# Moving a context norm one tile earlier and splitting its weight unit in two, in a two-block transformer kernel

## Chip, cores and metric

The kernel runs as one program on 1 core of one Trainium2 chip. The metric is device time in microseconds (us) of one launch; the median of the runs is compared.

## The reference, cut to what matters

A sequence of 512 rows of 1,024 channels goes through `first_block` (two layers, each attention and a gated feed-forward part of width 2,816) and `second_block`. All is computed in fp32. What the change touches is the border between the blocks:

```python
    return rmsnorm(x, g_final)                       # end of first_block
...
    h = modulate(rmsnorm_2(x, g_pre1[l]), sh1, sc1)      # second_block, x is that result
    hc = modulate(rmsnorm_2(ctx, g_pre1[l]), csh1, csc1) # ctx: 256 rows x 1024, an input
    q, k, v, f, g_a, g_f = split_proj(h @ w_in[l])
    pc = hc @ w_in[l, :, :Q_W + 2 * KV_W]                # only its k and v columns are used
```

## The kernel before, in words

Activations lie transposed in SBUF: 8 chunks of 128 channels by 512 rows. Every weight goes through one stream of units. For each unit the SP queue loads it into `raw` (2 slots), ScalarE (ACT) rounds it into `w_hi`, GpSimd (POOL) forms the rest `w_lo`, and TensorE (PE) forms three products per pair of 128x128 weights and activation chunk (hi by hi, hi by lo, lo by hi). `hi_unit` (L595) waits for the matmuls of the unit two before it; `L565` is POOL's part, `L1502` and `L1524` are the products. A unit is ready for PE when POOL has counted it (`unit_ready`).

The down projection `dn11` ends the first block: 8 units of 1,408 columns, each one output chunk of 33 matmuls. After each unit VectorE (DVE) adds the residual (L1175) and sums squares of the chunk twice: weighted, for the norm `pre1` (L1135, L1144), and plain, for the final norm (L1186 to L1189). The norm of the context is put among these units. In the ACT program, `context_rows`, and in DVE's, `context_part`, say what is done behind unit u: squares and their sum at u=1, a ones matmul on PE behind unit 2 (`context_sum`), root and inverse at u=3, and scaling, rounding (`ctx_hi`, L841) and rest (`ctx_lo`, L1161) from u=3 on. In `context_rows` each `next_hi` (the rounding of unit u+1) stands ahead of the context work of u, so work of u that waits for DVE delays the rounding of unit u+2.

Then comes the unit `ctx` (2,048 columns: 128 key and 128 value columns of 8 chunks). PE computes the context keys (24 matmuls of 256 columns), then the sums of the norm `pre1` (L1616, 16 matmuls of one column), the first value row tile (24 of 128 columns), the plain sums of the final norm (L1892, 8), the spread of the inverse of `pre1` over 128 partitions (L1623, 8), the second row tile, the spread of the final inverse (L1900, 8), and then unit 0 of `c_in` (48 matmuls of 512 columns, L1524), each of whose eight steps waits for a chunk `h_lo` of DVE (L996). ACT's `h_hi` (L646) of chunk 1 stands behind the copy of the second row tile (L913), and ahead of chunk 2 stands the rounding of unit 1 of `c_in`. Units 1 and 2 of `c_in` and the second block's attention follow.

Of the kernel before, what the change touches and what calls it, by code (L numbers as in the profile page):

```python
# [26 lines left out]
ACT = mybir.ActivationFunctionType  # L27
# [40 lines left out]
def constants():  # L68
# [14 lines left out]
    for name, head, rot in (("32", 128, 32), ("16", 64, 16)):  # L83
# [31 lines left out]
          ("up10", HALF, 2048, 2), ("dn10", 8, HALF * P, 1), ("up11", HALF, 2048, 2), ("dn11", 8, HALF * P, 1),  # L115
          ("ctx", 1, 2048, 3),
          ("c_in", 13, 2048, [2, 2, 5] + [2] * 10),
# [10 lines left out]
def lay_out(x):  # L128
# [31 lines left out]
    c = x["w_in_2"][0]  # L160
    w["ctx"] = units(c[:, 512:768], 256)
    cq = c[:, :512].reshape(D, 8, 64)[:, pair8].reshape(D, 512)
# [81 lines left out]
def program(nc, wdram, params_d, const_d, axial_d, rows_d, x_d, mem_d, ctx_d, cond_d, pos_d, out_d):  # L244
    ctx = ExitStack()
    with ctx:
# [80 lines left out]
        def bank(b, a=0, z=S):  # L327
            return ps[:, b * S + a:b * S + z]
# [255 lines left out]
        def _(act):  # L584
# [130 lines left out]

            def ffn_up(ph, first):
                def body(i, j):
                    next_hi(ph, i, j)

                    act.wait_ge(conv_ready, 2 * i + (j + 1 + first))  # L720
                    nc.scalar.activation(T[:, 2 + j, :], T[:, j, :], ACT.Silu).then_inc(silu_ready, 1)  # L721
                each_unit(act, ph.n, body)
# [104 lines left out]

            def context_rows():
                act.wait_ge(mod_used, 24)
                act.dma_start(CTXT[:], ctx_d).then_inc(load_ctx, 16)  # L830
                for u in range(8):
                    next_hi(PH["dn11"], u // 2, u % 2)
                    if u == 1:
                        act.wait_ge(load_ctx, 16)
                        nc.scalar.activation(CTXSQ[:], CTXT[:], ACT.Square).then_inc(ctx_squared, 1)
                    if u == 3:
                        act.wait_ge(ctx_summed, 1)
                        nc.scalar.activation(CTXR[:], bank(4, 0, MEM), ACT.Sqrt, bias=cst("eps"), scale=1.0 / D).then_inc(ctx_root, 1)
                    for k in range(3 * (u - 4), min(3 * (u - 3), DC)) if u >= 4 else []:
                        act.wait_ge(ctx_scaled, k + 1)  # L840
                        nc.scalar.activation(CTXH[:, k, :], CTXT[:, k, :], ACT.Identity, bias=MODV[:, k, 1:2]).then_inc(ctx_hi, 1)  # L841

            def ffn(l, first):
                for h in range(2):
                    name = f"dn{l}{h}"
                    mod = 8 * MOD_PHASES.index(name) if name in MOD_PHASES else None
                    if mod is not None:
                        if mod:
                            act.wait_ge(mod_used, mod)
                        load_mod(mod)  # L850
                        load_mod(mod + 1)
                    ffn_up(PH[f"up{l}{h}"], first + h * HALF)
                    if name == "dn11":
                        context_rows()
                        continue
                    if mod is None:
                        stream_only(PH[name])
                        continue
                    for u in range(8):
                        next_hi(PH[name], u // 2, u % 2)  # L860
                        if 2 <= u + 1 < 8:
                            act.wait_ge(mod_used, mod + u)
                            load_mod(mod + u + 1)
# [35 lines left out]
            ph = PH["ctx"]  # L899
            next_hi(ph, 0, 0)  # L900

            def after_pre1_root():
                act.wait_ge(final_summed, 1)
                nc.scalar.activation(ROOTF[:], bank(1, 0, ROWT), ACT.Sqrt, bias=cst("eps"), scale=1.0 / D).then_inc(final_root, 1)
                act.wait_ge(ph.done, 1)
                nc.scalar.activation(CKX[:], bank(2, 0, MEM), ACT.Copy).then_inc(ph.free, 1)
                act.wait_ge(ph.done, 2)
                nc.scalar.activation(CVX[:, 0, :], bank(3, 0, P), ACT.Copy).then_inc(ph.free, 1)

            def beside_pre1(k):  # L910
                if k == 1:
                    act.wait_ge(ph.done, 3)
                    nc.scalar.activation(CVX[:, 1, :], bank(0, 0, P), ACT.Copy).then_inc(ph.free, 1)  # L913
                if k == 2:
                    hi_unit(PH["c_in"], 0, 1)

            norm("pre1", None, None, free=[(PH["up11"].done, 22)], after_root=after_pre1_root, beside=beside_pre1,
# [59 lines left out]
        def _(v):  # L977
            chain = Chain(v, vec_steps)
            step = chain.step

            def norm(name, src, gain, shift=None, dst=(HH, HL), into=None, parts="scaled low", beside=None):
                i, nch, rows, b, s = NORMS[name]
# [20 lines left out]
                for k in range(nch if "scaled" in parts else 0):  # L1003
# [15 lines left out]
                    ins.then_inc(scaled_ready, 1)  # L1019
                    if k == 0 and beside is not None:  # L1020
                        beside()
                    if k >= 1 and "low" in parts:
# [127 lines left out]
            def context_part(u):  # L1150
                if u == 1:
                    v.wait_ge(ctx_squared, 1)
                    step(nc.vector.tensor_tensor(CTXSQ[:, 0:4, :], CTXSQ[:, 0:4, :], CTXSQ[:, 4:8, :], ALU.add))
                    step(nc.vector.tensor_tensor(CTXSQ[:, 0:2, :], CTXSQ[:, 0:2, :], CTXSQ[:, 2:4, :], ALU.add))
                    nc.vector.tensor_tensor(CTXSQ[:, 0, :], CTXSQ[:, 0, :], CTXSQ[:, 1, :], ALU.add).then_inc(ctx_added, 1)
                if u == 3:
                    v.wait_ge(ctx_root, 1)
                    step(nc.vector.reciprocal(CTXI[:], CTXR[:]))
                for k in range(3 * (u - 4), min(3 * (u - 3), DC)) if u >= 4 else []:
                    v.wait_ge(ctx_hi, k + 1)  # L1160
                    nc.vector.scalar_tensor_tensor(out=CTXL[:, k, :], in0=CTXT[:, k, :], scalar=MODV[:, k, 1:2],  # L1161
                                                   in1=CTXH[:, k, :].bitcast(F32), op0=ALU.add,
                                                   op1=ALU.subtract).then_inc(ctx_ready, 1)
                for k in range(3 * (u - 3), min(3 * (u - 2), DC)) if u >= 3 else []:
                    nc.vector.scalar_tensor_tensor(out=CTXT[:, k, :], in0=CTXT[:, k, :], scalar=DER[:, 1, k:k + 1],
                                                   in1=CTXI[:], op0=ALU.mult, op1=ALU.mult).then_inc(ctx_scaled, 1)
# [255 lines left out]

            def final_reciprocal():
                v.wait_ge(final_root, 1)
                nc.vector.reciprocal(INVF[:], ROOTF[:]).then_inc(final_inverse, 1)

            norm("pre1", lambda k: XT[:, k, :], lambda k: DER[:, 0, k:k + 1], shift=lambda k: MODV[:, k, 0:1],
                 beside=final_reciprocal)
            ph = PH["c_in"]
# [57 lines left out]
        def _(pe):  # L1487
# [337 lines left out]
            def context_sum(u):  # L1825
                if u == 2:
                    pe.wait_ge(ctx_added, 1)
# [55 lines left out]
            pe.wait_ge(ctx_ready, DC)  # L1883
            advance(t_tiles(ph, 0, (0,), (2,), rows=MEM, ah=CTXH, al=CTXL))
            rows = r_tiles(ph, 0, (0, 1), (3, 0), P, P, ah=CTXH, al=CTXL)

            def final_sums():
                advance(rows, 3 * DC)
                bank_free(1)
                pe.wait_ge(final_added, 1)  # L1890
                for t in range(ROWT):
                    ins = nc.tensor.matmul(bank(1, t, t + 1), T[:, 6, t * P:(t + 1) * P], ONES[:, 0:1], start=True, stop=True)  # L1892
                ins.then_inc(final_summed, 1)

            norm("pre1", after_sums=final_sums)
            advance(rows)
            bank_free(5)
            pe.wait_ge(final_inverse, 1)
            for t in range(ROWT):
                ins = nc.tensor.matmul(bank(5, t * P, (t + 1) * P), INVF[:, t:t + 1].broadcast_to([P, P]), cst("ident", P),  # L1900
                                       start=True, stop=True)
            ins.then_inc(final_spread, 1)
            last_read.update({0: (ph.free, 3), 1: (final_root, 1), 2: (ph.free, 1), 3: (ph.free, 2), 5: (x_ready, XR["final"] + DC)})
            ph = PH["c_in"]
            for u in range(3):
# [8 lines left out]
                else:  # L1914
                    advance(t_tiles(ph, u, (0, 1), (b, b + 1), ready=h_chunk("pre1") if u == 0 else None))
                    last_read[b], last_read[b + 1] = (ph.free, 2 * u + 1), (ph.free, 2 * u + 2)

            def c_rest():
# [93 lines left out]
```

## Time and profile before

| what | value |
|---|---|
| median of 3 runs | 2198.89 us (2198.7 to 2200.43) |
| profiled execution, its own time | 2199.97 us |
| its span, first to last instruction | 2198.2 us |
| PE busy | 2019.5 us, 92% of the span |
| DVE, POOL, ACT busy | 1146.2, 872.0 and 672.7 us |
| mean granted clock of TensorE | 0.963 |

In the timeline a line is one or several instructions of a group: start, time from the start of the first to the end of the last, engine, line, what it writes and reads, how many, and in brackets the idle time ahead of it and what ended it. A matmul's printed time contains its passage through the array, and matmuls overlap; their pace is the distance from start to start. 1.00 is a granted clock of 2.4 GHz, 0.50 is 1.2 GHz.

### The profile page before, as it was taken

How to read it: one execution, taken by the hardware profiler on the slowest of the kernel's cores; microseconds unless marked ns; L12 is line 12 of the kernel's file. 1: busy time of each engine (PE TensorE's matmuls, PEld its weight loads, DVE VectorE, ACT ScalarE, POOL GpSimd, SP SyncE). 2: the span in 40 equal slices, each digit the busy share in tenths (PEclk: the TensorE clock that was granted, in tenths of full speed). 3: DMA queues.
4: the chain of work that ended last, by engine and by line, in shares of the span. 5: the costliest groups of instructions: out<-in, count | busy, mean ns of one | idle time of the engine just before them, and what ended most of it. 6: DMA issues, size and time to landing. Idle time of an engine off the chain costs nothing.

```text
span 2198.2 us, 26021 instructions
## 1 busy us (share of the span) xinstructions
PE 2019.5 (92%) x9702; PEld 1613.7 (73%) x9702; DVE 1146.2 (52%) x2103; ACT 672.7 (31%) x1057; POOL 872.0 (40%) x648
## 2 busy tenths in 40 slices
PE   3988789999899988999999999999998969999997
PEld 3766467788688775567888887878876747888886
DVE  7777874535933766755434435762333455312334
ACT  4232562322122125552221222234434222212211
POOL 4343003444654641115445544442222323444442
PEclk9999999999999998999999999899999979999998
DMA  4222001422532431003325322221110212223221
GB/s 158 76 96 77 25 13 62 163 101 86 219 109 87 184 106 48 25 18 113 121 83 193 131 93 98 100 96 58 58 58 21 87 47 77 89 93 115 96 79 65
DMA packets 32062, 199.15 MB, mean 91 GB/s; under 512 B 3680, under 2 KB 3808, under 8 KB 14048
## 3 DMA queue, kind: packets, MB, share of 16 engines
q1 hardware_dynamic: 27072, 166.74, 21.6%
q10 hardware_dynamic: 4896, 31.15, 3.9%
q8 instruction: 60, 0.98, 0.2%
q14 instruction: 34, 0.28, 0.0%
HBM read 195.78 MB, written 2.10 MB: 90 GB/s over the span
## 4 chain that ended last, share of the span: by engine, by line
PE 49%; DVE 4%; ACT 1%; POOL 1%; issue 1%; DVEq 0%; ACTq 0%
PE psum L1502 42%; PE psum L1524 2%; PE psum L1695 1%; PE psum L1660 1%; PE psum L1677 1%; POOL w_lo L565 1%; PE psum L1952 1%; DVE xT L1012 1%; DVE work L1006 0%; PE psum L1632 0%; ACT w_hi L595 0%; PE psum L1623 0%; DVE work L1188 0%; DVE work L1017 0%; DVE work L1189 0%
## 5 line engine op out<-in xcount | busy, mean ns | idle before, releaser
L565 POOL TENSOR_TENSOR w_lo<-raw,w_hi 128x512 fp32r<-128x512 f32 (+2 forms) x640 | 863.7, 1379 | 1296.9 <-ACT w_hi L595 1296.9
L1502 PE MATMUL psum<-h_hi,w_hi 128*128 128x512 f32 x1560 | 616.0, 395 | 11.8 <-DVE a_q L1048 4.6
L1502 PE MATMUL psum<-h_hi,w_lo 128*128 128x512 f32 x1560 | 612.7, 393 | 0.0
L1502 PE MATMUL psum<-h_lo,w_hi 128*128 128x512 f32 x1560 | 612.4, 393 | 0.0
L595 ACT ACTIVATE w_hi<-raw 128x2048 fp32r<-128x2048 f32 (+2 forms) x176 | 301.6, 1714 | 566.3 <-PE psum L1502 471.9
L1502 PEld LDWEIGHTS psum<-h_hi,w_hi 128*128 128x128 f32 x1560 | 295.0, 189 | 85.1 <-issue 14.4
L1502 PEld LDWEIGHTS psum<-h_hi,w_lo 128*128 128x128 f32 x1560 | 294.7, 189 | 64.1 <-issue 2.4
L1502 PEld LDWEIGHTS psum<-h_lo,w_hi 128*128 128x128 f32 x1560 | 295.0, 189 | 62.4 <-issue 2.3
L1502 PE MATMUL psum<-g_hi,w_hi 128*128 128x512 f32 x528 | 207.5, 393 | 10.4 <-POOL w_lo L565 5.4
L1502 PE MATMUL psum<-g_hi,w_lo 128*128 128x512 f32 x528 | 205.6, 389 | 0.0
L1502 PE MATMUL psum<-g_lo,w_hi 128*128 128x512 f32 x528 | 205.5, 389 | 0.0
L1224 DVE TENSOR_SCALAR work<-psum,params 128x512 f32<-128x512 f32 x66 | 53.5, 810 | 221.0 <-PE psum L1502 212.8
L721 ACT ACTIVATE work<-work 128x512 f32<-128x512 f32 x66 | 41.8, 633 | 401.7 <-DVE work L1228 401.7
L1238 DVE TENSOR_TENSOR work<-psum,work 128x512 f32<-128x512 f32 x66 | 45.7, 692 | 173.9 <-PE psum L1502 170.8
L1502 PEld LDWEIGHTS psum<-g_hi,w_hi 128*128 128x128 f32 x528 | 99.1, 188 | 37.0 <-POOL w_lo L565 8.7
L1122 DVE CUSTOM_DVE_ANT_0 work_flat<-mod_w,conditions 128x1024 f32<-128x1024 f32 x64 | 115.6, 1807 | 1.6
L1502 PEld LDWEIGHTS psum<-g_hi,w_lo 128*128 128x128 f32 x528 | 99.1, 188 | 20.8
L1502 PEld LDWEIGHTS psum<-g_lo,w_hi 128*128 128x128 f32 x528 | 99.1, 188 | 20.1
L1228 DVE SCALAR_TENSOR_TENSOR work<-psum,params,work 128x511 f32<-128x511 f32 (+1 forms) x132 | 98.9, 750 | 15.3 <-DVE work L1224 1.1
L1175 DVE TENSOR_TENSOR xT<-psum,xT 128x512 f32<-128x512 f32 (+1 forms) x48 | 33.2, 691 | 135.0 <-PE psum L1502 134.8
L1524 PE MATMUL psum<-h_hi,w_hi 128*128 128x512 f32 x96 | 43.6, 455 | 50.4 <-DVE h_lo L1264 33.2
L1068 DVE CUSTOM_DVE_ANT_0 work_c<-psum,const 128x512 f32<-128x512 f32 (+1 forms) x32 | 23.0, 755 | 94.8 <-PE psum L1660 94.8
(312 smaller groups left out, 2478.7 us busy)
## 6 DMA issues: line engine op xcount, KB each, us to landing
raw<-w_up SPq DMA_DIRECT2D x66, 1024.0 KB, 4.8
raw<-w_dn SPq DMA_DIRECT2D x48, 704.0 KB, 4.1
mod_w<-w_mod ACTq DMA_DIRECT2D x24, 1024.0 KB, 4.9
raw<-w_c_in SPq DMA_DIRECT2D x13, 1024.0 KB, 4.8
raw<-w_b_in SPq DMA_DIRECT2D x7, 1024.0 KB, 4.8
raw<-w_a_idx SPq DMA_DIRECT2D x5, 1024.0 KB, 5.6
raw<-w_a_out SPq DMA_DIRECT2D x8, 640.0 KB, 3.8
raw<-w_b_out SPq DMA_DIRECT2D x8, 640.0 KB, 3.9
```

What stands on the lines that cost most here:

```text
L565: ins = nc.gpsimd.tensor_tensor(LO[slot][:, a:z], RAW[slot][:, a:z], HI[slot][:, a:z].bitcast(F32), ALU.subtract)
L595: nc.scalar.activation(HI[slot][:, 0:ph.size], RAW[slot][:, 0:ph.size], ACT.Copy).then_inc(hi_ready, 1)
L721: nc.scalar.activation(T[:, 2 + j, :], T[:, j, :], ACT.Silu).then_inc(silu_ready, 1)
L1012: nc.vector.tensor_tensor(XT[:, k, :], XT[:, k, :], out, ALU.add).then_inc(x_ready, 1)
L1068: ins = nc.vector.tensor_tensor_reduce(probs_of(s, n), src, st["mask"], 1.0, PICKED, ALU.add, ALU.max, o[:, n:n + 1])
L1122: ins = nc.vector.tensor_tensor_reduce(TW[:, 4 * S:4 * S + D], MODW[u % 2][:, c, :], COND[:, w, :], 1.0, 0.0, ALU.mult, ALU.add, MODV[:, 2 ...
L1175: nc.vector.tensor_tensor(d, bank(j), d, ALU.add).then_inc(ph.free, 1)
L1224: step(nc.vector.tensor_scalar(t, a, w(mid), w(3), ALU.mult, ALU.add))
L1228: ins = nc.vector.scalar_tensor_tensor(out=t[:, o], in0=a[:, s_], scalar=w(k), in1=t[:, o], op0=ALU.mult, op1=ALU.add)
L1238: nc.vector.tensor_tensor(g, b, T[:, 2 + j, :], ALU.mult).then_inc(ph.free, 1)
L1502: ins = nc.tensor.matmul(out, l, r, start=(k == 0 and m == 0), stop=(k == n - 1 and m == 2))
L1524: ins = nc.tensor.matmul(out, w, a, start=(k == 0 and m == 0), stop=(k == kc - 1 and m == 2))
```

## The change

The unit `ctx` becomes two units of 1,024 columns: keys, then values. The load of the context is issued by ACT ahead of the last SiLU of `up11`, where it stood behind it. Every step of the context norm moves one unit of `dn11` up: squares at u=0, the ones matmul behind unit 1, root and inverse at u=2, and so on. On PE the plain sums of the final norm move behind the second row tile (into bank 6), and the spread of the final inverse moves behind unit 0 of `c_in`. ACT takes the final root at chunk 4 of the norm `pre1`, and DVE the final reciprocal after the norm.

```diff
-          ("ctx", 1, 2048, 3),
+          ("ctx", 2, 1024, [1, 2]),
...
-    w["ctx"] = units(c[:, 512:768], 256)
+    w["ctx"] = units(c[:, 512:768], P)
...
-            def ffn_up(ph, first):
+            def ffn_up(ph, first, last=None):
                 def body(i, j):
                     next_hi(ph, i, j)
+                    if last is not None and isinstance(i, int) and 2 * i + j == ph.n - 1:
+                        last()
...
-            def context_rows():
+            def load_context():
                 act.wait_ge(mod_used, 24)
                 act.dma_start(CTXT[:], ctx_d).then_inc(load_ctx, 16)
+
+            def context_rows():
                 for u in range(8):
                     next_hi(PH["dn11"], u // 2, u % 2)
-                    if u == 1:
+                    if u == 0:
                         act.wait_ge(load_ctx, 16)
...
-                    if u == 3:
+                    if u == 2:
                         act.wait_ge(ctx_summed, 1)
...
-                    for k in range(3 * (u - 4), min(3 * (u - 3), DC)) if u >= 4 else []:
+                    for k in range(3 * (u - 3), min(3 * (u - 2), DC)) if u >= 3 else []:
                         act.wait_ge(ctx_scaled, k + 1)
...
             next_hi(ph, 0, 0)
+            next_hi(ph, 0, 1)
 
             def after_pre1_root():
-                act.wait_ge(final_summed, 1)
-                nc.scalar.activation(ROOTF[:], bank(1, 0, ROWT), ACT.Sqrt, bias=cst("eps"), scale=1.0 / D).then_inc(final_root, 1)
...
                 if k == 2:
                     hi_unit(PH["c_in"], 0, 1)
+                if k == 4:
+                    act.wait_ge(final_summed, 1)
+                    nc.scalar.activation(ROOTF[:], bank(6, 0, ROWT), ACT.Sqrt, bias=cst("eps"), scale=1.0 / D).then_inc(final_root, 1)
```

`context_part` on DVE has the same steps at u one lower, and the reciprocal for the final norm stands behind the norm `pre1`. On PE:

```diff
             def context_sum(u):
-                if u == 2:
+                if u == 1:
...
-            rows = r_tiles(ph, 0, (0, 1), (3, 0), P, P, ah=CTXH, al=CTXL)
-
-            def final_sums():
+            rows = r_tiles(ph, 1, (0, 1), (3, 2), 0, P, width=P, ah=CTXH, al=CTXL)
+
+            def first_rows():
+                unit_ready(ph, 1)
                 advance(rows, 3 * DC)
...
+            norm("pre1", after_sums=first_rows)
+            advance(rows)
+            last_read.update({2: (ph.free, 3), 3: (ph.free, 2)})
+            bank_free(6)
+            pe.wait_ge(final_added, 1)
+            for t in range(ROWT):
+                ins = nc.tensor.matmul(bank(6, t, t + 1), T[:, 6, t * P:(t + 1) * P], ONES[:, 0:1], start=True, stop=True)
...
                     advance(t_tiles(ph, u, (0, 1), (b, b + 1), ready=h_chunk("pre1") if u == 0 else None))
                     last_read[b], last_read[b + 1] = (ph.free, 2 * u + 1), (ph.free, 2 * u + 2)
+                    if u == 0:
+                        final_layout()
```

`final_layout` waits for `final_inverse` and issues the eight matmuls that spread it, which stood ahead of `c_in` before.

## Rows read from the trace of the kernel before

**Rows 1.** The page's chain that ended last, shares of the span by engine.

```profile
PE 49%; DVE 4%; ACT 1%; POOL 1%; issue 1%; DVEq 0%; ACTq 0%
```

**Rows 2.** Timeline of PE, the border of dn11 units 2 and 3, 6, 7, and ctx.

```profile
1363.23 0.39 PE L1502 MATMUL psum<-g_hi,w_lo 128*128 128x512 f32 x1
1365.16 0.70 PE L1829 MATMUL psum<-ctx_squares,ones 128*128 128x256 f32 x2 [1.54 <-DVE ctx_squares L1155]
...
1389.42 0.50 PE L1502 MATMUL psum<-g_hi,w_hi 128*128 128x512 f32 x1 [1.07 <-POOL w_lo L565]
...
1398.04 0.50 PE L1502 MATMUL psum<-g_hi,w_hi 128*128 128x512 f32 x1 [0.85 <-POOL w_lo L565]
...
1405.42 0.39 PE L1502 MATMUL psum<-g_hi,w_lo 128*128 128x512 f32 x1
1408.29 0.39 PE L1502 MATMUL psum<-ctx_hi,w_hi 128*128 128x256 f32 x1 [2.48 <-POOL w_lo L565]
```

**Rows 3.** Timelines of DVE, ACT and POOL over dn11; last the context's load (KB, us to landing).

```profile
1350.67 1.67 DVE L1186 TENSOR_TENSOR work<-xT 128x512 f32<-128x512 f32 x1
...
1362.69 1.23 DVE L1153 TENSOR_TENSOR ctx_squares<-ctx_squares 128x1024 f32<-128x1024 f32 x1
...
1373.49 0.69 DVE L1175 TENSOR_TENSOR xT<-psum,xT 128x512 f32<-128x512 f32 x1 [2.63 <-PE psum L1502]
...
1382.92 0.69 DVE L1175 TENSOR_TENSOR xT<-psum,xT 128x512 f32<-128x512 f32 x1
...
1399.77 0.68 DVE L1175 TENSOR_TENSOR xT<-psum,xT 128x512 f32<-128x512 f32 x1
...
1337.12 0.34 ACTq L830 DMA_DIRECT2D ctxT<-ctx_t  x1
...
1383.46 1.37 ACT L595 ACTIVATE w_hi<-raw 128x1408 fp32r<-128x1408 f32 x1
...
1400.30 1.91 ACT L595 ACTIVATE w_hi<-raw 128x2048 fp32r<-128x2048 f32 x1
...
1384.91 4.45 POOL L565 TENSOR_TENSOR w_lo<-raw,w_hi 128x512 fp32r<-128x512 f32 x3 [5.56 <-ACT w_hi L595]
...
ctxT<-ctx_t ACTq DMA_DIRECT2D x1, 1024.0 KB, 5.2
```

**Rows 4.** Timeline of PE from the context keys to unit 0 of c_in.

```profile
1409.46 0.28 PE L1502 MATMUL psum<-ctx_hi,w_hi 128*128 128x256 f32 x1
...
1412.46 2.15 PE L1616 MATMUL psum<-ones,work 128*128 128x1 f32 x16
1414.48 0.31 PE L1502 MATMUL psum<-w_hi,ctx_hi 128*128 128x128 f32 x1
...
1417.79 1.81 PE L1892 MATMUL psum<-ones,work 128*128 128x1 f32 x8
1419.46 2.05 PE L1623 MATMUL psum<-const,inverses 128*128 128x128 f32 x8
1421.16 0.45 PE L1502 MATMUL psum<-w_hi,ctx_hi 128*128 128x128 f32 x1
...
1426.32 2.02 PE L1900 MATMUL psum<-const,final_inverses 128*128 128x128 f32 x8
```

**Rows 5.** Windows: busy us of PE, PEld, DVE, ACT, POOL (with counts), granted clock, DMA share, GB/s.

```profile
1413.00:1416.40 3.40, 3.40 (x31) 3.40 (x32) 0.18 (x1) 0.26 (x1) 1.53 (x2) 0.98 0.23 41
1416.50:1428.00 11.50, 11.50 (x57) 11.50 (x56) 3.49 (x6) 2.87 (x7) 0.00 (x0) 0.50 0.20 79
1440.80:1467.80 27.00, 26.96 (x168) 24.01 (x167) 20.80 (x32) 4.68 (x5) 12.44 (x8) 1.00 0.22 78
```

**Rows 6.** Timeline of PE: the spread of the inverse in two other norms.

```profile
401.71 1.16 PE L1623 MATMUL psum<-const,inverses 128*128 128x128 f32 x8 [0.57 <-DVE inverses L986]
...
1783.08 2.08 PE L1623 MATMUL psum<-const,inverses 128*128 128x128 f32 x8 [0.56 <-DVE inverses L986]
```

**Rows 7.** Timeline of DVE: the first instruction that waits for unit 0 of c_in.

```profile
1440.20 0.01 DVE L1045 LOAD_MASK_SELECT work<-psum  x1 [1.59 <-PE psum L1524]
```

More of the change, by code:

```diff
@@ L851, in ffn @@
                         load_mod(mod + 1)
-                    ffn_up(PH[f"up{l}{h}"], first + h * HALF)
+                    ffn_up(PH[f"up{l}{h}"], first + h * HALF, load_context if name == "dn11" else None)
                     if name == "dn11":
@@ L912, in beside_pre1 @@
                     act.wait_ge(ph.done, 3)
-                    nc.scalar.activation(CVX[:, 1, :], bank(0, 0, P), ACT.Copy).then_inc(ph.free, 1)
+                    nc.scalar.activation(CVX[:, 1, :], bank(2, 0, P), ACT.Copy).then_inc(ph.free, 1)
                 if k == 2:
                     hi_unit(PH["c_in"], 0, 1)
+                if k == 4:
+                    act.wait_ge(final_summed, 1)
+                    nc.scalar.activation(ROOTF[:], bank(6, 0, ROWT), ACT.Sqrt, bias=cst("eps"), scale=1.0 / D).then_inc(final_root, 1)
             norm("pre1", None, None, free=[(PH["up11"].done, 22)], after_root=after_pre1_root, beside=beside_pre1,
@@ L979, in _, with norm @@
             step = chain.step
-            def norm(name, src, gain, shift=None, dst=(HH, HL), into=None, parts="scaled low", beside=None):
+            def norm(name, src, gain, shift=None, dst=(HH, HL), into=None, parts="scaled low"):
                 i, nch, rows, b, s = NORMS[name]
@@ L1019, in norm @@
                     ins.then_inc(scaled_ready, 1)
-                    if k == 0 and beside is not None:
-                        beside()
                     if k >= 1 and "low" in parts:
@@ L1150, in context_part @@
             def context_part(u):
-                if u == 1:
+                if u == 0:
                     v.wait_ge(ctx_squared, 1)
@@ L1155, in context_part @@
                     nc.vector.tensor_tensor(CTXSQ[:, 0, :], CTXSQ[:, 0, :], CTXSQ[:, 1, :], ALU.add).then_inc(ctx_added, 1)
-                if u == 3:
+                if u == 2:
                     v.wait_ge(ctx_root, 1)
                     step(nc.vector.reciprocal(CTXI[:], CTXR[:]))
-                for k in range(3 * (u - 4), min(3 * (u - 3), DC)) if u >= 4 else []:
+                for k in range(3 * (u - 3), min(3 * (u - 2), DC)) if u >= 3 else []:
                     v.wait_ge(ctx_hi, k + 1)
@@ L1163, in context_part @@
                                                    op1=ALU.subtract).then_inc(ctx_ready, 1)
-                for k in range(3 * (u - 3), min(3 * (u - 2), DC)) if u >= 3 else []:
+                for k in range(3 * (u - 2), min(3 * (u - 1), DC)) if u >= 2 else []:
                     nc.vector.scalar_tensor_tensor(out=CTXT[:, k, :], in0=CTXT[:, k, :], scalar=DER[:, 1, k:k + 1],
@@ L1421, in _ @@
             ffn(1, XT, ("add", "add"))
[L1423 to L1428, printed above, removed]
+            norm("pre1", lambda k: XT[:, k, :], lambda k: DER[:, 0, k:k + 1], shift=lambda k: MODV[:, k, 0:1])
+            v.wait_ge(final_root, 1)
+            nc.vector.reciprocal(INVF[:], ROOTF[:]).then_inc(final_inverse, 1)
             ph = PH["c_in"]
@@ L1883, in _, with final_layout @@
             pe.wait_ge(ctx_ready, DC)
-            advance(t_tiles(ph, 0, (0,), (2,), rows=MEM, ah=CTXH, al=CTXL))
-            rows = r_tiles(ph, 0, (0, 1), (3, 0), P, P, ah=CTXH, al=CTXL)
-            def final_sums():
-                advance(rows, 3 * DC)
-                bank_free(1)
-                pe.wait_ge(final_added, 1)
-                for t in range(ROWT):
[L1892 to L1903, printed above, removed]
+            advance(t_tiles(ph, 0, (0,), (2,), width=P, rows=MEM, ah=CTXH, al=CTXL))
+            last_read[2] = (ph.free, 1)
+            rows = r_tiles(ph, 1, (0, 1), (3, 2), 0, P, width=P, ah=CTXH, al=CTXL)
+            def first_rows():
+                unit_ready(ph, 1)
+                advance(rows, 3 * DC)
+            norm("pre1", after_sums=first_rows)
[5 more added lines that the diff above has]
+                ins = nc.tensor.matmul(bank(6, t, t + 1), T[:, 6, t * P:(t + 1) * P], ONES[:, 0:1], start=True, stop=True)
+            ins.then_inc(final_summed, 1)
+            last_read[6] = (final_root, 1)
+            def final_layout():
+                bank_free(5)
+                pe.wait_ge(final_inverse, 1)
+                for t in range(ROWT):
+                    ins = nc.tensor.matmul(bank(5, t * P, (t + 1) * P), INVF[:, t:t + 1].broadcast_to([P, P]), cst("ident", P),
+                                           start=True, stop=True)
+                ins.then_inc(final_spread, 1)
+                last_read[5] = (x_ready, XR["final"] + DC)
             ph = PH["c_in"]
@@ L1916, in _ @@
                     last_read[b], last_read[b + 1] = (ph.free, 2 * u + 1), (ph.free, 2 * u + 2)
+                    if u == 0:
+                        final_layout()
             def c_rest():
```

## Prediction, on record before the result

> **What bounds the kernel now.** I read the page's chain first [rows 1]. PE carries 49% of the span in the part that is followed and no other engine more than 4%, so a microsecond that PE loses is a microsecond of the kernel, unless another engine paces the stage. Then I read PE's timeline around the diff and looked for its idle brackets. There are four [rows 2]. 1.54 us before the ones matmul of the context norm, which waits for DVE's sum of squares; 1.07 and 0.85 us before units 6 and 7 of dn11; and 2.48 us before the context keys, the last three all waiting for POOL's low parts. Each idle stretch costs about 0.16 us more than its bracket, because matmuls that overlap (start to start 0.227 us) have to fill the array again: from 1405.42 to 1408.29 are 2.87 us where 0.23 would do, 2.64 lost.
>
> Third, the timelines of DVE, ACT and POOL say why POOL is late [rows 3]. From unit 3 on DVE does its residual work and the context's as well. One such round lasts 1382.92 - 1373.49 = 9.43 us with the inverse in it, and the next two (1399.77 - 1382.92)/2 = 8.4 us each, against 33 x 0.227 = 7.5 us of PE for a unit. ACT waits for DVE's scaled context chunks and rounds the next unit only then: at 1383.46, 2.5 us after unit 4 was done. Rounding 1.37 and POOL 4.45 us follow, and PE starts unit 6 late. The ctx unit is the third of these late ones, and the worst: rounding at 1400.30, 1.91 us for 2,048 columns, and four POOL pieces instead of three.
>
> Fourth, from the keys on PE is never idle until c_in, but it isn't always fast [rows 4, 5]. The granted clock is 0.98 between 1413.0 and 1416.4 and 0.50 from 1416.5 to 1428.0, where 128-column matmuls start every 0.213 us, and 1.00 in units 1 and 2 of c_in. There 168 matmuls take 27.0 us; without 72 of 512 columns (16.3 us) that leaves 0.111 us for each of the 96 of 128 columns. So the same matmul costs 0.111 or 0.213.
>
> **The change, step by step.**
>
> *Context load, squares, sum.* The load is issued about 6.4 us sooner (1330.7 for 1337.12) and takes 5.2 us, so it lands at about 1336, ahead of ACT's new square at 1341.6, behind the rounding of unit 1. DVE adds the squares at u=0, from 1350.67 + 1.67 = 1352.34. Alone the three adds take 2.4 us (1362.69 to 1365.1); beside POOL's pieces a DVE operation of this kind takes about 1 us more (1.67 for 0.69), once or twice here: done at 1355.8 to 1356.8, at worst 1357.6. PE asks at 1356.2. I take no wait; the bound is 1.4 us. The 1.54 us and their refill go: -1.7. If DVE were not idle in that round (2.2 us between its end and unit 1), the wait would only move.
>
> *The lag moves one unit up.* Unit 2 is now the one with the inverse behind it. It is done at about 1364.0, and the DVE round that began at 1373.49 begins at 1364.05, 9.44 us sooner. What followed it follows again: late roundings of units 5, 6 and 7. Units 5 and 6 lose what 6 and 7 lost (1.24 and 1.01). Unit 7 takes the place of ctx: rounding at 1400.30 - 9.44 = 1390.86, plus 1.37, 4.45 and 0.14 of handover is 1396.8, against unit 6 done at 1405.65 - 9.44 = 1396.2: 0.6 lost. dn11 ends at 1396.8 + 7.6 = 1404.4, where it ended at 1405.65: -1.2 in all (-1.7, +0.6, rounding).
>
> *The split unit.* Unit ctx 0 is rounded when unit 6 is done, and has half the columns: about 1.1 us of ACT and two POOL pieces of about 1.5, ready at about 1400.5, 4 us ahead of PE. The 2.48 us wait goes: -2.64. Unit ctx 1 may only be rounded when unit 7 is done: 1404.4 + 1.1 + 3.1 = 1408.7. PE wants it after keys and sums, 2.93 + 1.78 = 4.7 us after 1404.4, at 1409.1: no wait, at worst 0.4 with POOL slowed by DVE. The extra activation and DMA lie on ACT and SP, both idle there. ACT then rounds c_in 0 (1.9 us) when the keys are done, and the root of pre1 is queued behind that; the sums take 1.78, so the root is at most 0.3 late, and its result isn't needed for 3 more us. The first row tile covers it.
>
> *Clock of the keys.* Behind the idle 2.48 us the clock fell after a dozen of the 24 key matmuls: 4.17 us from 1408.29 to 1412.46, at a first pace of (1409.46 - 1408.29)/9 = 0.13 with the refill in it [rows 2, 4]. Without the gap I take 24 at 0.118 plus refill, 2.93: -1.24. Bound: 0, if the clock falls anyway. The sums take 16 x 0.111 = 1.78 for 2.02: -0.24.
>
> *Row tile 0.* 3.31 us before (1414.48 to 1417.79), 24 matmuls partly at full clock. The clock fell 4.0 us after the first sum. In two other norms the spread stands 3.3 and 3.6 us behind their first sum, and ran once fast (1.16 us) and once slow (2.08) [rows 6]. I take a fall 3.3 us behind the first sum, so 1.5 us into the tile: 13 x 0.111 + 11 x 0.213 = 3.8 us, +0.5. Bounds 2.67 (all fast) and 5.1 (all slow).
>
> *Plain sums.* They leave the place ahead of the spread: 1419.46 - 1417.79 = -1.67. They come back behind row tile 1, in the place that the final spread leaves (1.67 too), so PE reaches c_in as long after row tile 1 as before.
>
> *Spread and row tile 1.* 1.70 and 5.16 us at half clock, as before: 0.
>
> *Unit 0 of c_in.* ACT's h_hi of chunk 1 is still released by row tile 1, and from there DVE's 1.7 us a chunk set the pace; the end stays 13.8 us behind row tile 1 (1426.3 to 1440.2 [rows 4, 7]). ACT's new root at chunk 4 (0.26 us) fits in its idle of about 1 us a chunk. The final reciprocal comes after DVE's last chunk, 1.5 us before PE wants it. If PE had to wait for it, everything behind would.
>
> *Final spread behind unit 0.* New on the path between units 0 and 1, with nothing beside it: eight matmuls at full clock, 1.16 less the overlap: +1.0 (1.7 at half clock).
>
> Sum: -1.2 - 2.64 - 1.24 - 0.24 + 0.5 - 1.67 + 1.0 = -5.5 us. Behind it PE-bound units and the same attention follow and keep the shift. The profiled execution's 2199.97 (span 2198.2 and 1.8 around it) would become 2194.5; it lies 1.1 above the median, and from the median 2198.89 I get 2193.4.
>
> **A rule that speaks otherwise.** In the trace PE was busy for the whole of 1413.0 to 1416.4 and the clock fell right behind it [rows 5]. The Trainium skill ("TensorE: Matmul & The Clock Gate", "HAM oscillation — how this bites in real kernels") puts the fall down to idle stretches of PE. By that rule the new kernel, which has none behind dn11, would keep the full clock; by the row, a stretch full of one-column and 128-column matmuls is enough for the fall. That is the second case below.
>
> **Rivals.**
> 1. *The clock holds through both row tiles.* For it: 96 such matmuls run at 1.00 in c_in, and the stretch before the sums is now dense. Against: rows 5, a fall with no idle time. Price: row tile 0 2.67, spread 1.0, row tile 1 2.67, so -0.64, -0.7, -2.49 in place of +0.5: -9.8, 2189.1.
> 2. *The clock falls already in the sums.* Row tile 0 takes 5.1 (+1.8), the sums +0.5: -3.4, 2195.5; if the keys are slow too, and the sums take 3.4 us, -1.3, 2197.6. For it: the fall before came at a time that I can't place, and the spread at 1783.08 was slow.
> 3. *The lag isn't moved but grows*: DVE's adds at u=0 hold PE 1.4 us, and ctx 1 is 0.4 late: -3.7, 2195.2.
> 4. *Slower.* The low clock doesn't lift in c_in: each 512-column matmul costs 0.427 for 0.227. It takes 50 of them to turn -5.5 into more than +4.4; for units 0 and 1 together it is about +12, 2211. Against: the window of units 1 and 2 at 1.00, behind a low stretch longer than the new one.
>
> **How the numbers follow.** The forecast's own case (2191.5 to 2195) 50%; rival 1 20%; rivals 2 and 3 24% together; rival 4 and anything like it 6%. 0.2% is 4.4 us, about what a measurement of this kernel tells from no change: 2194.5 and 2203.3. The forecast's case lies below 2194.5 in five of six, rival 1 wholly, rivals 2 and 3 in one of five: faster 0.67, same 0.28, slower 0.05. The range 2188.0 to 2197.6 takes in rival 1 and the bounds of 2 and 3.
>
> **What would show it.** Right: no idle bracket before the ones matmul and before the keys; brackets of about 1.1, 0.85 and 0.4 before units 5, 6 and 7; dn11 ending at about 1404.4; keys in 2.9 us; row tile 1 done at about 1419.8; clock 0.50 there; c_in unit 1 starting 5.5 us sooner. Wrong: a bracket before ctx 1's row tile or the final spread, 128-column matmuls at 0.111 in both tiles, or a shift that is lost behind c_in.

## The result, and the profile after

| | before | after |
|---|---|---|
| median | 2200.43 us (5 runs, 2198.7 to 2204.39) | 2188.43 us (5 runs, 2184.2 to 2193.81) |
| ratio after/before | | 0.9943, 95% interval 0.9922 to 0.9964 |
| profiled execution: span, clock | 2198.2 us, 0.963 | 2182.4 us, 0.972 |

The kernel became 12 us faster; the forecast was 5.5. (Taken from the ratio it is 12.5 us, and its interval goes from 8 to 17.) A second measurement, below, gave 9.2 us.

PE's timeline of the changed kernel, in the places of [rows 2]: the ones matmul, the late units of dn11, and the keys.

```profile
1335.57 0.47 PE L1503 MATMUL psum<-g_hi,w_hi 128*128 128x512 f32 x1 [0.83 <-issue]
...
1351.17 0.70 PE L1830 MATMUL psum<-ctx_squares,ones 128*128 128x256 f32 x2 [0.36 <-DVE ctx_squares L1159]
...
1375.41 0.50 PE L1503 MATMUL psum<-g_hi,w_hi 128*128 128x512 f32 x1 [1.07 <-POOL w_lo L565]
...
1384.03 0.50 PE L1503 MATMUL psum<-g_hi,w_hi 128*128 128x512 f32 x1 [0.85 <-POOL w_lo L565]
...
1392.27 0.50 PE L1503 MATMUL psum<-g_hi,w_hi 128*128 128x512 f32 x1 [0.47 <-POOL w_lo L565]
...
1399.66 0.39 PE L1503 MATMUL psum<-g_hi,w_lo 128*128 128x512 f32 x1
1399.89 0.28 PE L1503 MATMUL psum<-ctx_hi,w_hi 128*128 128x256 f32 x1
...
1402.76 1.84 PE L1617 MATMUL psum<-ones,work 128*128 128x1 f32 x16
1404.52 0.33 PE L1503 MATMUL psum<-w_hi,ctx_hi 128*128 128x128 f32 x1
...
1407.25 1.11 PE L1624 MATMUL psum<-const,inverses 128*128 128x128 f32 x8
1408.11 0.30 PE L1503 MATMUL psum<-w_hi,ctx_hi 128*128 128x128 f32 x1
...
1410.83 1.00 PE L1899 MATMUL psum<-ones,work 128*128 128x1 f32 x8
1411.69 0.48 PE L1525 MATMUL psum<-h_hi,w_hi 128*128 128x512 f32 x1
...
1425.08 1.05 PE L1907 MATMUL psum<-const,final_inverses 128*128 128x128 f32 x8
1425.89 0.48 PE L1503 MATMUL psum<-h_hi,w_hi 128*128 128x512 f32 x1
```

The keys follow dn11 without a gap (1399.66 to 1399.89, where [rows 2] have 2.87 us). The brackets of 1.07 and 0.85 stand one unit earlier than in [rows 2], and a third of 0.47 stands before unit 7. From the keys on, everything is at the fast pace: keys 2.87 us, sums 1.76, row tiles 2.73 and 2.72 (3.31 and 5.16 in [rows 4]), spread and plain sums 0.86 each (1.70 and 1.67). Two windows over this stretch, columns as in [rows 5]:

```profile
1399.90:1411.70 11.80, 11.80 (x106) 11.80 (x104) 7.87 (x9) 5.17 (x9) 8.17 (x6) 1.00 0.33 109
1411.70:1425.90 14.20, 13.08 (x59) 9.51 (x58) 11.20 (x16) 6.85 (x10) 6.38 (x4) 1.00 0.38 142
```

The granted clock is 1.00 where [rows 5] have 0.50.

**How to count.** Of the 15.8 us between the two profiled spans a part lies in code that the change doesn't touch. The clearest place is the attention of the first block's second layer, some 400 us ahead of the change. Windows over the same work, the kernel before first, then after:

```profile
803.00:974.00 171.00, 151.00 (x930) 102.77 (x929) 116.18 (x426) 92.60 (x288) 31.33 (x23) 0.92 0.09 31
```

```profile
802.60:968.70 166.10, 146.08 (x928) 99.73 (x926) 115.56 (x426) 92.44 (x288) 31.32 (x23) 0.95 0.09 32
```

4.9 us there, at a clock of 0.92 and 0.95. Over the 13 profiles of this study dn11 begins anywhere between 1333.6 and 1342.5 us, though the work ahead of it is the same. So I measure the **stage**, from the first matmul of dn11 unit 0 to the first of c_in unit 1, in each profile: 99.68 us before (1340.93 to 1440.61), 90.32 after (1335.57 to 1425.89). The change is worth 9.4 us there, which lies within the interval of 8 to 17. The rest of the first measurement's 12 lies outside the stage, and I put it down to the spread of the executions.

### The profile page after: what moved, and what is told of

It is laid out like the page before. It is cut to its first block, busy times and chain, and to the rows that moved or that the text cites. A ratio compares the mean times of both kernels' runs of the same rounds, so it can differ in the third digit from the quotient of the medians.

```text
span 2182.4 us, 26025 instructions
## 1 busy us (share of the span) xinstructions
PE 2004.0 (92%) x9702; PEld 1599.0 (73%) x9702; DVE 1145.2 (52%) x2103; ACT 672.2 (31%) x1058; POOL 871.9 (40%) x648
## 4 chain that ended last, share of the span: by engine, by line
PE 49%; DVE 4%; ACT 1%; POOL 1%; issue 1%; DVEq 0%; ACTq 0%
PE psum L1503 42%; PE psum L1525 2%; PE psum L1696 1%; PE psum L1678 1%; PE psum L1661 1%; POOL w_lo L565 1%; PE psum L1962 1%; DVE xT L1018 1%; DVE work L1012 0%; PE psum L1633 0%; ACT w_hi L595 0%; PE psum L1624 0%; DVE work L1023 0%; DVE h_lo L1002 0%; PE psum L1617 0%
## 5 line engine op out<-in xcount | busy, mean ns | idle before, releaser
L595 ACT ACTIVATE w_hi<-raw 128x2048 fp32r<-128x2048 f32 (+3 forms) x177 | 301.6, 1704 | 569.3 <-PE psum L1503 474.9
```

Source lines behind the costliest of these rows:

```text
L595: nc.scalar.activation(HI[slot][:, 0:ph.size], RAW[slot][:, 0:ph.size], ACT.Copy).then_inc(hi_ready, 1)
```

## Experiments

Times are medians minus the median of the kernel before, measured beside it on the same chip; the stage is read from each run's one profile. "Tile 0" and "tile 1" are the two value row tiles, and all lengths are in us.

| run | what | idle before keys | keys | tile 0 | tile 1 | stage | time against before, us; ratio's interval |
|---|---|---|---|---|---|---|---|
| before | | 2.48 | 4.17 | 3.31 | 5.16 | 99.68 | |
| after | | 0 | 2.87 | 2.73 | 2.72 | 90.32 | -12.0; 0.9922 to 0.9964 |
| e1 | after again | 0 | 2.88 | 2.74 | 2.71 | 90.27 | -9.2; 0.9946 to 0.9973 |
| e2 | norm up alone | 0.53 | 2.98 | 2.77 | 5.16 | 95.29 | -3.6; 0.9973 to 0.9991 |
| e3 | split alone | 0.56 | 2.94 | 3.24 | 5.16 | 96.16 | -3.4; 0.9969 to 0.9988 |
| e4 | sums last alone | 2.49 | 4.19 | 3.31 | 2.93 | 96.56 | -2.3; 0.9979 to 0.9997 |
| e5 | after without split | 0.51 | 2.98 | 2.92 | 3.32 | 92.67 | -6.5; 0.9954 to 0.9980 |
| e6 | after, old order of sums | 0 | 2.87 | 2.73 | 2.71 | 90.39 | -9.5; 0.9937 to 0.9966 |
| e7 | after, gap of 4.4 | 4.43 | 4.36 | 2.71 | 2.71 | 96.33 | -3.1; 0.9980 to 0.9999 |
| e8 | after, ctx_hi later | 0 | 2.87 | 2.71 | 2.72 | 86.94 | -14.1; 0.9918 to 0.9949 |
| e9 | after, gap of 0.9 | 0.90 | 2.93 | 3.17 | 3.07 | 93.01 | -6.6; 0.9957 to 0.9981 |
| e10 | after, gap of 1.7 | 1.69 | 2.94 | 3.90 | 5.15 | 97.82 | -3.7; 0.9980 to 0.9999 |
| e11 | e2 again | 0.51 | 2.98 | 2.89 | 5.16 | 95.40 | -9.9, one execution only |

### e1 to e4: the change again, and its three parts

e1 is the changed kernel, unedited. e2, e3 and e4 are the kernel before with one part of the change each, cut out of its diff:

```diff
# e2: the context norm one unit up, and its load (as in context_rows, context_part, context_sum)
-                if u == 2:
+                if u == 1:
                     pe.wait_ge(ctx_added, 1)
# e3: the unit in two
-          ("ctx", 1, 2048, 3),
+          ("ctx", 2, 1024, [1, 2]),
# e4: plain sums behind row tile 1, final spread behind c_in unit 0, root and reciprocal to match
-                bank_free(1)
-                pe.wait_ge(final_added, 1)
...
+                    if u == 0:
+                        final_layout()
```

> The changed kernel once more. The stage is counted from the first matmul of dn11 unit 0 to the first of c_in unit 1: 99.7 us before, 90.3 after in the profiled executions. Theory A (the idle gap before the keys is what let the clock fall, and without it the clock holds): stage 90.3 again, granted clock 1.00 from the keys to c_in, kernel about 9 us below the one before. Theory B (the clock in this stage is a matter of where in time it lies; the first profile was lucky): the clock falls in the sums or row tiles in some executions, stage 94 to 95, kernel 5 to 6 us below. In both, brackets of 1.07, 0.85 and 0.47 us before dn11 units 5, 6 and 7.

> The kernel before with only the context norm one unit up (and its load sooner). The one ctx unit of 2,048 columns would be ready at about the end of dn11, so the gap of 2.48 us before the keys nearly goes. Theory A: the clock holds, keys 2.9, sums 1.8, two row tiles 2.7 each, plain sums and spread 0.9 each: stage 89.7, kernel 10 us faster than before. Theory B: dn11 -1.2 and gap -2.6 only, stage 95 to 96, kernel 4 us faster, unless by chance.

> The kernel before with only the unit ctx in two. The low part for the keys is ready at about the end of dn11, but the last two ctx_lo of DVE end 1.4 us later, so a gap of 1 to 1.4 us stays in place of 2.48, and the ones matmul still waits 1.54. Own ledger: -1.2 us, stage 98.5 if the clock falls as before. Theory A leaves it open whether half the gap is enough for a fall; if not, stage 91 to 92. Theory B: either, by chance.

> The kernel before with only the order of the final norm's matmuls changed (plain sums behind the second row tile, final spread behind c_in unit 0). The gap of 2.48 us before the keys stays. Theory A: the clock falls in the keys or the tiles as before, stage 99.7 - 1.7 + 1.0 = 99.0, kernel within 1 us of the one before. Theory B: by chance the clock holds, stage 93 to 94.

e1: stage 90.27, clock 1.00 again, 9.2 us. Theory B's bad case didn't show in this profile.

e2 speaks against theory A as I had worded it. Only half a microsecond of the gap was left, and the clock fell all the same. Its timeline, then its windows up to the fall and behind it:

```profile
1407.42 0.39 PE L1506 MATMUL psum<-ctx_hi,w_hi 128*128 128x256 f32 x1 [0.53 <-POOL w_lo L565]
...
1410.40 1.84 PE L1620 MATMUL psum<-ones,work 128*128 128x1 f32 x16
...
1414.88 1.81 PE L1896 MATMUL psum<-ones,work 128*128 128x1 f32 x8
1416.55 2.06 PE L1627 MATMUL psum<-const,inverses 128*128 128x128 f32 x8
```

```profile
1407.40:1414.80 7.40, 7.38 (x64) 7.38 (x65) 3.52 (x5) 1.85 (x3) 5.44 (x4) 1.00 0.40 142
1414.90:1425.00 10.10, 10.10 (x48) 10.10 (x48) 3.40 (x6) 2.77 (x7) 0.00 (x0) 0.50 0.28 106
```

PE is busy for all of both windows. The clock is 1.00 up to row tile 0 and 0.50 from the plain sums on. Where the same matmuls take 0.86 us after the change, they take 1.67.

e3: the gap went from 2.48 to 0.56, and the stage was 96.16 where I had 98.5 (I had put the gap at 1 to 1.4: with half the columns POOL was done ahead of DVE's last two ctx_lo, which took 0.88 us where they had taken 2.81 beside it). A fall again, in row tile 0. e4 beat its ledger by 2.4 us: the clock fell in the keys and in row tile 0 as before, but row tile 1 took 2.93 us where I had 5.16. By the medians each part alone is worth 2.3 to 3.6 us, 9.3 together, but they aren't independent: in the stage they give 4.4, 3.5 and 3.1, 11.0 together, where the whole change gives 9.4.

### e5 to e8: pairs of parts, a gap put back, a later ctx_hi

e5 is e2 and e4 together, e6 is e2 and e3 together. e7 and e8 are the changed kernel with one edit each:

```diff
# e7, PE ahead of the keys
-            unit_ready(ph, 0)
+            unit_ready(ph, 1)
             pe.wait_ge(ctx_ready, DC)
# e8, ACT in context_rows
-                    for k in range(3 * (u - 3), min(3 * (u - 2), DC)) if u >= 3 else []:
+                    for k in range(3 * (u - 4), min(3 * (u - 3), DC)) if u >= 4 else []:
                         act.wait_ge(ctx_scaled, k + 1)
```

> The changed kernel without the split: context norm one unit up and the matmuls of the final norm last, one ctx unit of 2,048 columns. Theory A (the gap alone decides) fell with the norm moved alone: no gap, and the clock fell all the same, behind the eight plain sums. Theory C: the clock holds only if both are gone, the gap before the keys and the plain sums between row tile and spread. C expects here a short gap of 0.5 us before the keys and the clock at 1.00: stage 90.9, kernel 9 us below before. If the split itself matters (theory D: four sparse steps fit only into the shorter stage of the split kernel), stage 94 to 95.

> The changed kernel with the old order of the final norm's matmuls: plain sums between row tile 0 and the spread, final spread ahead of c_in. No gap before the keys. Theory C: keys, sums and row tile 0 fast, then a fall at the plain sums and 5.2 us for row tile 1: stage 94.8, kernel 5 us below before. Theory D: the clock holds, stage 89.7.

> The changed kernel, but PE waits for the low part of the second ctx unit ahead of the keys: an idle gap of about 4.3 us, nothing else changed. Theory C: the gap brings back the fall: keys 4.2 instead of 2.9, sums 2.0, row tile 0 3.3, spread 1.7, and row tile 1 2.9 as with the sums last alone, so stage 90.3 + 4.4 + 1.3 + 0.3 + 0.6 + 0.8 + 0.2 = 97.9. If a gap doesn't matter: 94.7, clock 1.00.

> The changed kernel with ACT's ctx_hi of each group one step later (behind the rounding of the next unit instead of ahead of it). If the wait of ACT for DVE is what makes the roundings late, the brackets of 1.07, 0.85 and 0.47 us before dn11 units 5, 6 and 7 go, and DVE, still about 1.9 us late with the last residual, costs the sums at most 0.7: stage 87.5 to 88.2, kernel 2 to 3 us below the changed one. If POOL or DVE paces dn11 in another way, the brackets stay or move. The clock should hold.

Theory C fell. e6 has the plain sums in their old place, 24 one-column matmuls within 5.4 us, and stays at full speed; e5 has them last, and slows down (tiles 2.92 and 3.32). The rows are e6's:

```profile
1408.70 1.84 PE L1621 MATMUL psum<-ones,work 128*128 128x1 f32 x16
...
1413.20 1.00 PE L1898 MATMUL psum<-ones,work 128*128 128x1 f32 x8
1414.06 1.14 PE L1628 MATMUL psum<-const,inverses 128*128 128x128 f32 x8
```

What e5 has and e6 hasn't is 0.51 us of idle time before the keys. The same holds for e2 against e6. So either the gap or the split unit decides; D and A were left.

e7, with 4.43 us of idle time:

```profile
1406.88 0.58 PE L1503 MATMUL psum<-ctx_hi,w_hi 128*128 128x256 f32 x1 [4.43 <-POOL w_lo L565]
```

```profile
1406.90:1411.20 4.30, 4.30 (x24) 4.30 (x25) 0.47 (x1) 0.00 (x0) 0.00 (x0) 0.63 0.69 244
1411.30:1420.00 8.70, 8.70 (x81) 8.70 (x80) 3.08 (x5) 4.00 (x8) 4.97 (x4) 1.00 0.08 10
```

The keys ran slow, and then the clock came back and stayed through sums, spread and both tiles. I had expected all of them slower, and a stage of 97.9; it was 96.33. So the long gap cost 4.6 us for itself and 1.5 in the keys, and less behind them than half a microsecond of gap did in e2.

e8: no wait of PE is listed between the ones matmul and c_in, the three brackets are gone. The stage is 86.94 us (I had 87.5 to 88.2), 3.4 below the changed kernel; the sums weren't held up by DVE either. Its median is 2185.50 us against 2199.58 for the kernel before (ratio 0.9933). That it is faster than the changed kernel rests on the stage: the two were never measured side by side, and the intervals of their ratios to the kernel before overlap.

### e9 to e11: a short gap in the changed kernel, and e2 again

```diff
# e9
             unit_ready(ph, 0)
+            pe.wait_ge(PH["dn11"].free, 8)
# e10
             unit_ready(ph, 0)
+            pe.wait_ge(square_ready, NORMS["pre1"][3] + 1)
```

> The changed kernel, but PE waits ahead of the keys for DVE's residual of the last dn11 unit, an idle gap of about 0.75 us and nothing else. So far each profile with idle time before the keys (0.5 to 4.4 us, five kernels and the one before) shows the clock at 0.50 somewhere between keys and c_in, and each of the four profiles without it shows 1.00. If a short gap is enough (theory A): a fall at or behind the sums as in the kernels with 0.5 us, stage 90.3 + 0.9 + 1.5 to 4.4 = 92.7 to 95.6. If it isn't the gap but the split unit (theory D): stage 91.2, clock 1.00.

> The changed kernel, but PE waits ahead of the keys for the squares of the last chunk, an idle gap of about 1.6 us. Theory A: a fall, in the keys or behind the sums, stage 90.3 + 1.8 + 1.3 to 4.4 = 93.4 to 96.5. Theory D: stage 92.1, clock 1.00.

> The kernel with only the context norm moved up, once more, for a second profile. Its first showed a gap of 0.53 us before the keys and a fall between row tile 0 and the plain sums that lasted until c_in, stage 95.3. Theory A: a fall again, stage 93 to 96. If the fall is a matter of where in time the stage lies, it may hold this time: stage 90.0 to 90.9.

e9, timeline and windows:

```profile
1406.08 0.36 PE L1503 MATMUL psum<-ctx_hi,w_hi 128*128 128x256 f32 x1 [0.90 <-issue]
...
1409.01 1.84 PE L1617 MATMUL psum<-ones,work 128*128 128x1 f32 x16
...
1413.89 2.02 PE L1624 MATMUL psum<-const,inverses 128*128 128x128 f32 x8
```

```profile
1406.10:1412.50 6.40, 6.40 (x56) 6.40 (x57) 4.20 (x4) 2.66 (x5) 4.43 (x4) 1.00 0.27 91
1412.60:1419.40 6.80, 6.80 (x49) 6.80 (x48) 2.91 (x4) 1.57 (x4) 3.60 (x3) 0.75 0.43 147
```

With the split and everything else of the change in place, 0.90 us of idle time brought the fall back, behind the sums: stage +2.7, of which 1.1 is the gap and its refill. e10, with 1.69 us, fell too and stayed low to c_in:

```profile
1410.00:1413.30 3.30, 3.30 (x32) 3.30 (x31) 0.82 (x2) 2.43 (x4) 0.85 (x2) 1.00 0.62 204
1413.40:1416.80 3.40, 3.40 (x18) 3.40 (x17) 0.00 (x0) 0.28 (x1) 3.40 (x4) 0.50 0.23 96
```

Its stage is +7.5, 1.3 above the range I had given it. Theory D is out. e11 began dn11 8.8 us earlier in the execution than e2 and shows the same: full speed up to row tile 0, then a fall that lasts, stage 95.40 against 95.29. So it isn't where in the execution the stage lies. (Its -9.9 us is one execution, whose dn11 begins 7.3 us earlier than in the profile of the kernel before; it measures nothing of the edit.)

All nine profiles with idle time before the keys (0.51 to 4.43 us) show a fall between the keys and c_in; all four without it (after, e1, e6, e8) show none.

Two things in these profiles don't fit a fall that simply follows the gap. First, in the six with 0.51 to 1.69 us of idle time (e2, e3, e5, e9, e10, e11) the first fall stands 72.2 us behind the first matmul of dn11, to 0.1 us, whatever the gap: 7.3 us behind the gap's end in e2, 6.0 in e10. The profiles of after, e1 and e6 run through the same 72.2 us at full clock. What PE has done by then differs: the sums begin 67.2 us behind dn11's first matmul in those three, and 67.9 to 69.1 in the six. A wait leaves PE idle, and it also moves all the work behind it; no run here does one without the other. e11 doesn't either, for its fall stands at the same distance from dn11 as e2's.

Second, in e4, e7 and e9 the clock fell once more near the start of c_in, 13.4 to 15.1 us behind the gap, with PE busy all that time and the clock back at 1.00 ahead of it. Windows up to that fall and behind it in e4 and e9, and behind it in e7:

```profile
1420.80:1424.10 3.30, 3.30 (x31) 3.30 (x31) 2.80 (x4) 1.38 (x3) 0.00 (x0) 1.00 0.02 5
1424.30:1427.50 3.20, 3.20 (x8) 2.51 (x8) 2.23 (x3) 3.20 (x5) 1.30 (x2) 0.50 0.01 3
```

```profile
1416.40:1419.60 3.20, 3.20 (x31) 3.20 (x31) 2.46 (x4) 1.49 (x3) 0.00 (x0) 1.00 0.68 215
1419.80:1423.10 3.30, 3.30 (x9) 2.56 (x8) 2.39 (x3) 3.09 (x4) 1.51 (x2) 0.50 0.24 97
```

```profile
1420.40:1423.60 3.20, 3.20 (x9) 2.44 (x8) 2.29 (x3) 3.09 (x4) 1.41 (x2) 0.50 0.70 292
```

These falls cost nothing: from the end of row tile 1 to the end of c_in unit 0 are 14.2 to 14.3 us in these three, as in the changed kernel.

## Why the prediction was wrong

The direction was right, and so was the ledger of waits but for one of 0.36 us; the sum was -5.5 and the stage gave -9.4. Step by step:

- **Context load, squares, sum**: I took no wait, with a bound of 1.4 us. DVE's three adds took 4.1 us beside POOL for 2.4 alone, and PE waited 0.36 us. Cost with refill: 0.5. dn11 as a whole became 0.4 us shorter, not 1.2.
- **The lag moves one unit up**: predicted brackets of 1.07, 0.85 and 0.4 before units 5, 6 and 7; measured 1.07, 0.85, 0.47. e8 shows its cause: ACT's wait for DVE standing ahead of the rounding. With the two swapped they are gone.
- **The split unit**: the 2.48 us gap is gone, and PE didn't wait for the second unit (the row tile starts 1.76 us behind the sums).
- **Clock of the keys**, -1.24 predicted, -1.30 measured; the sums 1.76 for 1.78.
- **Row tile 0, spread, row tile 1** are the step that failed. "I take a fall 3.3 us behind the first sum", and half clock for spread and tile 1. No fall came: 2.73, 0.86 and 2.72 us for 3.8, 1.70 and 5.16. These three terms are 4.35 us. With dn11 (+0.8) and the smaller matters they lead from -5.5 to -9.4. The three places that the fall was taken from all have idle time of PE close ahead: 2.48 us before the keys, and brackets of 0.57 and 0.56 us before the spreads of [rows 6]. The new kernel has none from dn11 unit 7 on.
- **Plain sums, c_in unit 0, final spread**: row tile 1 to the end of c_in unit 0 took 14.3 us before and after; the final spread cost 0.81 for 1.0; the root at chunk 4 and the late reciprocal cost nothing.
- The last 2.6 us to the 12 of the first measurement are no part of the change: e1 repeats it at 9.2.

I had read from [rows 5] that a clock may fall while PE is busy, and concluded that sparse matmuls were enough for it, whatever the gap ahead of the keys. That conclusion was wrong, not the row: e9 and e10 put nothing but a wait ahead of the keys back, and the fall came back. Rival 1 named the case that came, at 20%, and priced it at -9.8. (Rival 2's first sum is off by its own terms: -3.7, not -3.4.)

The rule that I set against the trace, the Trainium skill's "TensorE: Matmul & The Clock Gate" ("HAM oscillation — how this bites in real kernels"), gave the right side for the changed kernel: no idle stretch, no fall, and the granted clock is 1.00 from 1399.90 to 1425.90. The trace doesn't bear it out as the whole story: in e2 and e9 the clock fell 7.3 and 6.8 us after a short gap, and in e4, e7 and e9 13 to 15 us after one, with PE busy all the time in between.

**What stays open.** Why a gap of 0.5 us has its effect only behind the sparse one-column sums, why one of 4.4 us leaves sums and tiles alone and is followed by a fall only behind the last eight sums, and why moving the plain sums shortens a fall (row tile 1 2.93 for 5.16 in e4 against before, 3.32 for 5.16 in e5 against e2) but makes no difference without one (e6). The runs show that a fall between keys and c_in goes with a wait before the keys in 13 profiles of 13, and that a wait alone brings it (e9, e10). They don't show whether it acts through PE's idle time or because it moves the sums and tiles to a later time. What would tell is a run that delays the sums with dense matmuls in place of a wait; there is none. The changed kernel and e2 have two profiles each and the others one, so how long a fall lasts may vary from one execution to another. Only the profiled executions can be read that closely: of the others there is a mean clock alone.

## What to carry to other kernels

Where a dense stretch of matmuls is followed by sparse ones (sums of one column, short tiles), price a small wait ahead of them by more than its bracket: put into the changed kernel, waits of 0.9 and 1.7 us lengthened the stage by 2.7 and 7.5 us, most of it through the clock. When a profile shows a low clock with PE busy, look for idle time some microseconds further back before calling the fall independent of it.

In an in-order queue that serves two streams, put the instruction that waits for the slower engine behind the one that feeds PE. In e8 that was one line, and worth another 3.4 us of the stage.

## What was not expected of the hardware

- The granted clock fell to 0.50 some 7 us after an idle stretch of only 0.5 to 0.9 us, PE busy throughout (e2, e9: 7.3 and 6.8 us), and came back within the keys after one of 4.43 us (e7: 0.63 over the keys, then 1.00 for the next 10 us).
- The first fall stood 72.2 us behind dn11's first matmul in six profiles, though their gaps went from 0.51 to 1.69 us.
- The clock fell from 1.00 to 0.50 behind 13 to 15 us in which PE was never idle (e4, e7, e9).
- Unchanged work ahead of the change differed by up to 8.9 us between executions (dn11 begins at 1333.6 to 1342.5), of which the attention windows above show 4.9 us at 0.92 and 0.95.
